# Differential attention in a fused two-block kernel: a head's sum of squares put on all partitions by one product with ones, and a wide root on ScalarE

## The chip, the cores and the metric

The kernel runs on one core of a Trainium2 chip. The metric is the device time of one execution in microseconds (us). Engines are named as in the profile: PE is TensorE (PEld its weight loads), DVE is VectorE, ACT is ScalarE, POOL is GpSimd, SP is SyncE, which issues the weight transfers.

## What is computed

Two blocks of a model on 512 tokens and 1024 channels. The first has a pooling, a gated recurrence and a stick-breaking attention branch and a feed-forward part. The second has two layers; the first of them mixes a state-space branch and a differential attention with 8 heads of width 128. The change is inside this differential attention:

```python
def diff_attention_group(q, k, v, pos, layer, lambdas, subln):
    ...
    def block(start, q1b, q2b):
        mask = chunk_causal_mask(start, s)
        p1 = masked_softmax(jnp.einsum('bqhd,bkhd->bhqk', q1b, k1, ...) * scale, mask)
        p2 = masked_softmax(jnp.einsum('bqhd,bkhd->bhqk', q2b, k2, ...) * scale, mask)
        return jnp.einsum('bhqk,bkhe->bqhe', p1 - lam * p2, vf)

    o = sweep_query_blocks(block, q[:, :, :, 0], q[:, :, :, 1])
    o = rms_norm_2(o, subln) * (1.0 - lam_init)
```

`rms_norm_2` divides each token's 128 values of a head by the root of their mean square. That norm of `o` is what is changed.

## The kernel before

All engines run programs written out by hand; each instruction order is fixed, and engines meet at counted semaphores. Dense products are fp32 work made of three TensorE products of split operands (`L617`, `L618`, `L619`; for value tiles `L638` to `L640`). Every weight panel goes SP transfer, ScalarE cast to `w_hi` (`L1290`, in `hi_to`), GpSimd subtraction to `w_lo` (`L588`, two instructions for a panel of 1024 columns), TensorE.

In the differential attention there are 32 steps c, four query blocks i = 0 to 3 for each of 8 heads. On TensorE (`attend_diff`) a step is: some units of the dense "fill" (the projections of later heads, then the output product `out2a`), the score products of step c + 1 (`L970`, `L973`), more fill, the transposes of step c (`L1015`). Scores of c + 1 wait for ScalarE's exponentials of step c. VectorE takes maxima (`L2304`, `L2305`), ScalarE the exponentials (`L1594`), VectorE normalises and subtracts (`L2338` to `L2341`), then does what the fill has finished (`beside_diff`: rotary products `L2258`, `L2260`, `L2261`, or `L2316`, `L2318` for `out2a`), then the next maxima.

A head's output is made during the steps of the next head, head numbers 0 to 7 here:

- step i = 0: `value_sums` on TensorE (`L984`) writes the head's output, channels on partitions and 512 tokens along the row, into PSUM bank 7. It waits until the head before has left the bank (`s_yb`). ScalarE squares it into `T[:, 0]` (`L1602`) and copies it to `T[:, 1]` (`L1606`).
- step i = 1: `square_sum` (`L992`): for each of four blocks of tokens a product whose held operand is the 128 x 128 block of squares and whose moving operand is one column of ones, so that a sum stands on its token's partition, 128 x 4 in all. ScalarE, in `head_root`, turns them into 1/root by Ln and Exp on 128 x 4 (`L1612`, `L1613`), in `cols`.
- step i = 2: `root_spread` (`L998`): four products of a column of `cols`, repeated, with the identity. They put the 1/root of every token on all partitions, in bank 7.
- step i = 3: `head_out` on VectorE: `L2309` multiplies `T[:, 1]` with a column and with bank 7, and `split` (`L1843`, `L1844`) rounds the result into the two operands of `out2b`.

Head 7 has no next head; after step 31 TensorE does `value_sums(7)`, three units of fill, `square_sum(7)`, three units, `root_spread(7)`, the rest of the fill, and then `out2b`, whose first two tiles wait for banks that VectorE frees at `L2317` after `L2316` and, in their last unit, for head 7's split.

Of the kernel before, what the change touches and what calls it, by code (L numbers as in the profile page):

```python
# [12 lines left out]
ACT = mybir.ActivationFunctionType  # L13
AX = mybir.AxisListType

P = 128
# [3 lines left out]
ST = S // P  # L20
# [211 lines left out]
def run(fill, n):  # L232

    for _ in range(n):
        if next(fill, fill) is fill:
            return
# [19 lines left out]
def build(nc, xt, weights, vectors, late, consts, masks, w_gates, positions, out):  # L256

    ctx = ExitStack()
    with ctx:
# [3 lines left out]
        def sem(name):  # L263
            return ctx.enter_context(nc.semaphore(name))
# [10 lines left out]
        T = sb("T", [P, 4, S])  # L275
# [3 lines left out]
        small = sb("small", [P, 256])  # L279
        cols = sb("cols", [P, 24])  # L280
# [11 lines left out]
        ps = ctx.enter_context(nc.psum_tensor("ps", [P, 8, S], F32))  # L292
# [5 lines left out]
        def con(name, rows=slice(0, P)):  # L298
            at, n = CCOL[name]
            return C_[rows, at:at + n]  # L300
# [151 lines left out]
        def lvec(name, i=0, n=1):  # L452
# [47 lines left out]
        s_ang, s_sin = sem("angles_ready"), sem("sines_ready")  # L500
        s_qc, s_vd, s_rot, s_rotf, s_roped = (sem("qk_copied"), sem("v_copied"), sem("rotated"), sem("rotated_read"),
                                              sem("roped"))
        s_sc, s_mx, s_ex, s_pn, s_tr, s_pt, s_dv, s_osq, s_os, s_or, s_osp, s_og, s_yb = (
            sem("scores_ready"), sem("max_ready"), sem("exp_ready"), sem("probs_ready"), sem("probs_turned"),
            sem("probs_copied"), sem("dv_ready"), sem("o_squares"), sem("o_sum"),
            sem("o_rms"), sem("o_spread"), sem("o_copied"), sem("y_diff_ready"))
        s_s5p, s_s5a, s_s5t, s_s5w, s_bu, s_buf, s_tab, s_tabx, s_ys, s_s5z = (
            sem("s5_params"), sem("s5_params_act"), sem("s5_turned"), sem("s5_in_weights"), sem("bu_ready"),
            sem("bu_read"), sem("table_angles"), sem("tables_ready"), sem("s5_out_ready"),
# [91 lines left out]
        def _(pe):  # L601
            mm_ = nc.tensor.matmul
# [105 lines left out]
            fill = token_units(("v_a", 0), HX)  # L708
# [4 lines left out]
            fill = token_units(("v_a", 1), HX)  # L713
# [228 lines left out]
            fill = chain(fill_dqkv(0), fill_dqkv(1))  # L942
            segments(0)
            for s in range(32):
                pair, i = divmod(s, 4)
# [42 lines left out]
            def square_sum(head):  # L988
                pe.wait_ge(s_osq, head + 1)
                pe.wait_ge(s_og, head + 1)  # L990
                for b in range(ST):
                    mm = mm_(ps[:, 7, b:b + 1], T[:, 0, P * b:P * b + P], con("ones")[:, 0:1], start=True, stop=True)  # L992
                mm.then_inc(s_os, 1)

            def root_spread(head):
                pe.wait_ge(s_or, head + 1)
                for b in range(ST):
                    mm = mm_(ps[:, 7, P * b:P * b + P], cols[:, 12 + b:13 + b].to_broadcast([P, P]), con("ident"),  # L998
                             start=True, stop=True)
                mm.then_inc(s_osp, 1)  # L1000

            def attend_diff(fill):
                scores(0)
                for c in range(32):
                    head, i = c // 4, c % 4
                    n = DIFF_FILL[c % len(DIFF_FILL)]
                    run(fill, n // 2)
                    if c + 1 < 32:
                        scores(c + 1)
                    run(fill, n - n // 2)  # L1010
                    pe.wait_ge(s_pn, c + 1)
                    if c:
                        pe.wait_ge(s_pt, c)
                    for kb in range(i + 1):
                        mm = nc.tensor.transpose(ps[:, 6, P * kb:P * kb + P], EX[:, 2 * (c % 2), P * kb:P * kb + P],  # L1015
                                                 con("ident"))
                    mm.then_inc(s_tr, 1)
                    if i == 0 and head:
                        value_sums(head - 1)
                    if i == 1 and head:  # L1020
                        square_sum(head - 1)
                    if i == 2 and head:
                        root_spread(head - 1)

            def fill_out():
                pe.wait_ge(s_ya, 8)
# [7 lines left out]
            value_sums(7)  # L1034
            run(fill, 3)
            square_sum(7)
            run(fill, 3)
            root_spread(7)
            run(fill, 1000)
            together("out2b", (0, 1), YB, (s_yb, 0))  # L1040
            for t in range(2, 8):
# [198 lines left out]
            fill = fill_mla()  # L1240
# [40 lines left out]
        def _(act):  # L1281
# [316 lines left out]
            def head_squares(head):  # L1598
                act.wait_ge(s_dv, head + 1)
                if head:  # L1600
                    act.wait_ge(s_os, head)
                link(A_(T[:, 0, :], ps[:, 7, :], ACT.Square))  # L1602
                act.sem_inc(s_osq, 1)
                if head:
                    act.wait_ge(s_yb, head)
                link(nc.scalar.copy(T[:, 1, :], ps[:, 7, :]))  # L1606
                act.sem_inc(s_og, 1)

            def head_root(head):

                act.wait_ge(s_os, head + 1)
                link(A_(cols[:, 12:16], ps[:, 7, 0:4], ACT.Ln, bias=con("eps"), scale=1.0 / P))  # L1612
                A_(cols[:, 12:16], cols[:, 12:16], ACT.Exp, scale=-0.5).then_inc(s_or, 1)  # L1613

            exponentials(0)
            for c in range(32):
# [214 lines left out]
        def _(dve):  # L1831
            link = Link(dve, v_own)
            v = nc.vector
# [471 lines left out]
                v.tensor_scalar(small[:, b:b + 2], small[:, b:b + 2], -0.125, None, ALU.mult).then_inc(s_mx, 1)  # L2305

            def head_out(head):
                dve.wait_ge(s_osp, head + 1)
                link(v.scalar_tensor_tensor(T[:, 3, :], T[:, 1, :], small[:, 63:64], ps[:, 7, :],  # L2309
                                            ALU.mult, ALU.mult))  # L2310
                split(YB, head, T[:, 3, :], s_yb)

# [451 lines left out]
```

## Time and profile before

| | us |
|---|---|
| median of 3 runs | 2564.46 (2559.68 to 2565.71) |
| the profiled execution, its own time | 2565.91 |
| its span, first to last instruction | 2564.1 |
| PE busy | 2482.4 (97%) |
| DVE busy | 1310.1 (51%) |
| ACT busy | 868.5 (34%) |
| POOL busy | 1059.6 (41%) |

The differential attention takes from about 1306 us of the span, with the first maximum, to about 1515 us, with the first product of `out2b`. A time such as 1353.15 below is always us from the span's start. In a timeline row the second number is the duration; "x8" on a TensorE fp32 row counts two records for each product in the code.

### The profile page before, as it was taken

What the parts mean: (1) busy time and instruction counts of PE and PEld (TensorE: products, weight loads), DVE (VectorE), ACT (ScalarE), POOL (GpSimd) and SP (SyncE); (2) the same over time, 40 slices, a digit from 0 to 9 for tenths busy, and PEclk for the clock granted to TensorE, in tenths of its full rate; (3) what the DMA queues carried; (4) which work ended last, traced back from release to release, by engine and by line L of the source; (5) the groups of instructions that cost most, each with busy time, mean ns of one, the idle gap of its engine ahead of it and who ended that gap; (6) DMA issues with size and microseconds to landing.
All of it is one profiled execution on the core that took longest, in us unless ns stands there. A gap on an engine that the chain in (4) does not pass through costs nothing.

```text
span 2564.1 us, 30219 instructions
## 1 busy us (share of the span) xinstructions
PE 2482.4 (97%) x11742; PEld 1982.0 (77%) x11742; DVE 1310.1 (51%) x1960; ACT 868.5 (34%) x1360; POOL 1059.6 (41%) x830
## 2 busy tenths in 40 slices
PE   7999999999999999999989999999999889999998
PEld 6887767888888888876667778888888656788886
DVE  6336687543533321584756655596127855533301
ACT  4453345322322222334444433222224443322221
POOL 4322244544544444453222235454454222544442
PEclk9999999999999999999999999999999989999999
DMA  4212122322322233221111123232231012222232
GB/s 147 66 58 72 56 72 89 99 96 93 103 99 95 94 99 98 92 74 58 58 42 50 50 72 106 99 99 94 93 105 54 28 34 63 98 94 95 96 98 78
DMA packets 62574, 209.45 MB, mean 82 GB/s; under 512 B 6880, under 2 KB 9184, under 8 KB 62304
## 3 DMA queue, kind: packets, MB, share of 16 engines
q1 hardware_dynamic: 61424, 204.11, 24.3%
q10 hardware_dynamic: 1008, 3.41, 0.4%
q8 instruction: 94, 1.54, 0.3%
q14 instruction: 48, 0.39, 0.0%
HBM read 205.39 MB, written 2.10 MB: 81 GB/s over the span
## 4 chain that ended last, share of the span: by engine, by line
PE 86%; DVE 10%; ACT 2%; issue 1%; DMA 0%; DVEq 0%; ACTq 0%; SPq 0%
PE ps L617 24%; PE ps L619 24%; PE ps L618 24%; DVE T L2157 1%; PE ps L638 1%; PE ps L639 1%; PE ps L640 1%; PE ps L956 1%; PE ps L733 1%; ACT A L1594 1%; PE ps L725 1%; PE ps L970 1%; PE ps L984 1%; PE ps L754 1%; PE ps L756 1%
## 5 line engine op out<-in xcount | busy, mean ns | idle before, releaser
L588 POOL TENSOR_TENSOR w_lo<-w_raw,w_hi 128x512 fp32r<-128x512 f32 (+4 forms) x822 | 1049.9, 1301 | 1465.8 <-ACT w_hi L1290 1465.8
L617 PE MATMUL ps<-H,w_hi 128*128 128x512 f32 x1880 | 750.6, 399 | 22.6 <-DVEq L1852 12.9
L619 PE MATMUL ps<-H,w_lo 128*128 128x512 f32 x1880 | 736.5, 392 | 0.0
L618 PE MATMUL ps<-H,w_hi 128*128 128x512 f32 x1880 | 736.0, 391 | 0.0
L1290 ACT CAST w_hi<-w_raw 128x1024 fp32r<-128x1024 f32 (+4 forms) x411 | 403.0, 984 | 526.1 <-DMA w_raw<-in_weights_dram 519.7
L617 PEld LDWEIGHTS ps<-H,w_hi 128*128 128x128 f32 x1880 | 355.7, 189 | 110.4 <-issue 21.3
L617 PE MATMUL ps<-split,w_hi 128*128 128x512 f32 x1034 | 410.4, 397 | 6.9 <-issue 3.7
L619 PEld LDWEIGHTS ps<-H,w_lo 128*128 128x128 f32 x1880 | 355.2, 189 | 75.3
L618 PEld LDWEIGHTS ps<-H,w_hi 128*128 128x128 f32 x1880 | 355.9, 189 | 71.2 <-issue 1.7
L619 PE MATMUL ps<-split,w_lo 128*128 128x512 f32 x1034 | 404.2, 391 | 0.0
L618 PE MATMUL ps<-split,w_hi 128*128 128x512 f32 x1034 | 403.7, 390 | 0.0
L1875 DVE TENSOR_TENSOR T<-ps,R 128x512 f32<-128x512 f32 x164 | 113.4, 692 | 405.3 <-PE ps L619 400.9
L617 PEld LDWEIGHTS ps<-split,w_hi 128*128 128x128 f32 x1034 | 194.9, 189 | 49.9 <-issue 7.7
L619 PEld LDWEIGHTS ps<-split,w_lo 128*128 128x128 f32 x1034 | 194.8, 188 | 41.3
L618 PEld LDWEIGHTS ps<-split,w_hi 128*128 128x128 f32 x1034 | 195.0, 189 | 40.0 <-issue 1.4
L1882 DVE TENSOR_TENSOR X<-X,ps 128x512 f32<-128x512 f32 x48 | 33.0, 687 | 331.4 <-PE ps L619 329.8
L1304 ACT ACTIVATE SQ<-X 128x512 f32<-128x512 f32 x49 | 31.0, 632 | 211.7 <-DVEq L1884 198.7
L1477 ACT ACTIVATE T<-T 128x512 f32<-128x512 f32 x66 | 41.7, 632 | 167.7 <-DVEq L2124 167.6
L2127 DVE TENSOR_TENSOR T<-T 128x512 f32<-128x512 f32 x66 | 81.8, 1239 | 9.7
L638 PE MATMUL ps<-w_hi,H 128*128 128x256 f32 x256 | 76.9, 300 | 0.0
L639 PE MATMUL ps<-w_lo,H 128*128 128x256 f32 x256 | 72.7, 284 | 0.0
L640 PE MATMUL ps<-w_hi,H 128*128 128x256 f32 x256 | 72.6, 283 | 0.0
(408 smaller groups left out, 2423.2 us busy)
## 6 DMA issues: line engine op xcount, KB each, us to landing
w_raw<-in_weights_dram SPq DMA_DIRECT2D x323, 512.0 KB, 3.6
w_raw<-in_weights_dram SPq DMA_DIRECT2D x48, 448.0 KB, 3.2
w_raw<-in_weights_dram SPq DMA_DIRECT2D x22, 256.0 KB, 2.6
X<-in_xt_dram SPq DMA_DIRECT2D x4, 512.0 KB, 7.9
out_dram<-A SPq DMA_DIRECT2D x8, 256.0 KB, 2.1
w_raw<-in_weights_dram SPq DMA_DIRECT2D x12, 128.0 KB, 2.0
w_raw<-in_weights_dram SPq DMA_DIRECT2D x6, 192.0 KB, 2.3
A<-in_w_gates_dram ACTq DMA_DIRECT2D x1, 1024.0 KB, 4.8
```

The costliest lines, as they stand in the source:

```text
L588: sub = nc.gpsimd.tensor_tensor(w_lo[:, p % NS, c], w_raw[:, p % NS, c], w_hi[:, p % NS, c].bitcast(F32), ALU.subtract)
L617: mm_(ps[:, bank, :], r(wh), xh, start=(k == 0), stop=False)
L618: mm_(ps[:, bank, :], r(wh), xl, start=False, stop=False)
L619: mm = mm_(ps[:, bank, :], r(wl), xh, start=False, stop=(k == kt - 1))
L638: mm_(o, xh, r(wh), start=(k == 0), stop=False)
L639: mm_(o, xh, r(wl), start=False, stop=False)
L640: mm = mm_(o, xl, r(wh), start=False, stop=(k == kt - 1))
L1290: nc.scalar.copy(w_hi[:, p % NS, 0:PSIZE[p]], w_raw[:, p % NS, 0:PSIZE[p]]).then_inc(w_hi_ready[p % NS], 1)
L1477: A_(T[:, j % 2, :], T[:, j % 2, :], ACT.Silu).then_inc(s_silu, 1)
L1875: link(v.tensor_tensor(dst, ps[:, bank, :], R, ALU.mult))
L1882: link(v.tensor_tensor(X[:, t, :], X[:, t, :], ps[:, bank, :], ALU.add))
L2127: link(v.tensor_tensor(T[:, 2 + q, :], T[:, 2 + q, :], T[:, q, :], ALU.mult))
```

## The change

`square_sum` becomes one product: the held operand is the 128 x 128 block of ones, the moving operand the 512 columns of squares. Every partition then has the sum of every token. ScalarE's Ln and Exp work on 128 x 512, in place in `T[:, 0]`. `root_spread` and its semaphore are gone, and `head_out` reads the root from `T[:, 0]` in SBUF, not from PSUM. Since `T[:, 0]` now lives until `head_out`, `head_squares` waits for `s_yb` before its first instruction; `value_sums`, which it waits for anyway, has already waited for the same count.

```diff
             def square_sum(head):
                 pe.wait_ge(s_osq, head + 1)
                 pe.wait_ge(s_og, head + 1)
-                for b in range(ST):
-                    mm = mm_(ps[:, 7, b:b + 1], T[:, 0, P * b:P * b + P], con("ones")[:, 0:1], start=True, stop=True)
-                mm.then_inc(s_os, 1)
-
-            def root_spread(head):
-                pe.wait_ge(s_or, head + 1)
-                for b in range(ST):
-                    mm = mm_(ps[:, 7, P * b:P * b + P], cols[:, 12 + b:13 + b].to_broadcast([P, P]), con("ident"),
-                             start=True, stop=True)
-                mm.then_inc(s_osp, 1)
+                mm_(ps[:, 7, :], con("ones"), T[:, 0, :], start=True, stop=True).then_inc(s_os, 1)
...
                     if i == 1 and head:
                         square_sum(head - 1)
-                    if i == 2 and head:
-                        root_spread(head - 1)
...
             square_sum(7)
-            run(fill, 3)
-            root_spread(7)
             run(fill, 1000)
...
             def head_squares(head):
                 act.wait_ge(s_dv, head + 1)
                 if head:
-                    act.wait_ge(s_os, head)
+                    act.wait_ge(s_yb, head)
                 link(A_(T[:, 0, :], ps[:, 7, :], ACT.Square))
                 act.sem_inc(s_osq, 1)
-                if head:
-                    act.wait_ge(s_yb, head)
...
                 act.wait_ge(s_os, head + 1)
-                link(A_(cols[:, 12:16], ps[:, 7, 0:4], ACT.Ln, bias=con("eps"), scale=1.0 / P))
-                A_(cols[:, 12:16], cols[:, 12:16], ACT.Exp, scale=-0.5).then_inc(s_or, 1)
+                link(A_(T[:, 0, :], ps[:, 7, :], ACT.Ln, bias=con("eps"), scale=1.0 / P))
+                A_(T[:, 0, :], T[:, 0, :], ACT.Exp, scale=-0.5).then_inc(s_or, 1)
...
             def head_out(head):
-                dve.wait_ge(s_osp, head + 1)
-                link(v.scalar_tensor_tensor(T[:, 3, :], T[:, 1, :], small[:, 63:64], ps[:, 7, :],
+                dve.wait_ge(s_or, head + 1)
+                link(v.scalar_tensor_tensor(T[:, 3, :], T[:, 1, :], small[:, 63:64], T[:, 0, :],
                                             ALU.mult, ALU.mult))
```

TensorE's program at two places of one head in the second half, the sum of squares and, a step later, the place where the root was spread (`C_` holds the constants, the changed kernel's lines are numbered lower):

```order
 L618 MATMUL ps<-H,w_hi 128x512
 L619 MATMUL ps<-H,w_lo 128x512
-L1015 MATMUL ps<-C_,A 128x128 x2
-L992 MATMUL ps<-C_,T 128x1 x4
+L1006 MATMUL ps<-C_,A 128x128 x2
+L991 MATMUL ps<-T,C_ 128x512
...
-L1015 MATMUL ps<-C_,A 128x128 x3
-L998 MATMUL ps<-C_,cols 128x128 x4
+L1006 MATMUL ps<-C_,A 128x128 x3
```

Four products of one column become one of 512 columns, the four of the spread go, and nothing else on TensorE moves.

ScalarE's program before, around head 1's root, with what is queued behind it up to the next exponentials:

```order
576 L1594 ACTIVATE A,small<-ps,small 128x384 x2
577 L1625 COPY A<-ps 128x2x128
578 L1612 ACTIVATE cols<-ps,C_ 128x4
579 L1613 ACTIVATE cols<-cols 128x4
580 L1290 CAST w_hi<-w_raw 128x1024
581 L1354 ACTIVATE A<-ps,cols 128x256 x4
582 L1290 CAST w_hi<-w_raw 128x1024
583 L1594 ACTIVATE A,small<-ps,small 128x512 x2
```

and the same rows of the changed kernel:

```order
576 L1581 ACTIVATE A,small<-ps,small 128x384 x2
577 L1610 COPY A<-ps 128x2x128
578 L1597 ACTIVATE T<-ps,C_ 128x512
579 L1598 ACTIVATE T<-T 128x512
580 L1277 CAST w_hi<-w_raw 128x1024
581 L1341 ACTIVATE A<-ps,cols 128x256 x4
582 L1277 CAST w_hi<-w_raw 128x1024
583 L1581 ACTIVATE A,small<-ps,small 128x512 x2
```

The order is the same; two instructions of 4 columns have 512.

VectorE's program of the changed kernel from head 6's output on, at the end of the attention:

```order
1056 L2303 TENSOR_TENSOR X<-X,A 128x512
1057 L2294 SCALAR_TENSOR_TENSOR T<-T,small 128x512
1058 L1828 CAST split_5253<-T 128x512
1059 L1829 TENSOR_TENSOR split_5235<-T,split_5253 128x512
1060 L2301 TENSOR_TENSOR A<-ps,R 128x512
1061 L2303 TENSOR_TENSOR X<-X,A 128x512
1062 L2294 SCALAR_TENSOR_TENSOR T<-T,small 128x512
1063 L1828 CAST split_5262<-T 128x512
1064 L1829 TENSOR_TENSOR split_5244<-T,split_5262 128x512
1065 L2301 TENSOR_TENSOR A<-ps,R 128x512
```

Only the operands of rows 1057 and 1062 differ from before: there `ps` was read as well, now both tensors are in `T`, in SBUF.

## Rows read from the trace of the kernel before

**Rows 1.** The page, part 4: who holds the chain that ended last

```profile
PE 86%; DVE 10%; ACT 2%; issue 1%; DMA 0%; DVEq 0%; ACTq 0%; SPq 0%
```

**Rows 2.** Timeline of TensorE, heads 0 and 1: start, duration, line, shape

```profile
1345.80 1.02 PE L906 MATMUL ps<-A,C_ 128*128 128x512 f32 x2
1346.65 0.38 PE L1015 MATMUL ps<-C_,A 128*128 128x128 f32 x2
...
1353.15 1.06 PE L998 MATMUL ps<-C_,cols 128*128 128x128 f32 x8
1353.96 0.36 PE L638 MATMUL ps<-w_hi,H 128*128 128x256 f32 x1
```

**Rows 3.** The chain in order of time: head 2's square sum

```profile
1394.20 0.79 PE ps L992 x8
```

**Rows 4.** ScalarE: head 0's root in the timeline

```profile
1348.37 0.27 ACT L1612 ACTIVATE cols<-ps,C_ 128x4 f32<-128x4 f32 x1
1348.67 0.20 ACT L1613 ACTIVATE cols<-cols 128x4 f32<-128x4 f32 x1
```

**Rows 5.** ScalarE lines of width 512: ns min/median/max

```profile
L1309 ACT ACTIVATE R<-ps,C_ x3: 688/688/688, 689.9 to 2202.5; 128x512 f32<-128x512 f32 x3
L1477 ACT ACTIVATE T<-T x66: 631/632/635, 695.0 to 2426.4; 128x512 f32<-128x512 f32 x66
```

**Rows 6.** Timeline, head 0: GpSimd, VectorE, and TensorE's next scores

```profile
1350.66 3.15 POOL L588 TENSOR_TENSOR w_lo<-w_raw,w_hi 128x512 fp32r<-128x512 f32 x2 [8.21 <-ACT w_hi L1290]
1351.01 1.67 DVE L2261 TENSOR_TENSOR A<-A 128x512 f32<-128x512 f32 x1
1356.34 0.49 PE L970 MATMUL ps<-A 64*128 64x128 f32 x4 [0.70 <-ACTq L1596]
```

**Rows 7.** Timeline, head 1: ScalarE's exponentials and TensorE's next scores

```profile
1377.24 0.68 ACT L1594 ACTIVATE A<-ps,small 128x512 f32<-128x512 f32 x1
1378.71 0.19 ACT L1594 ACTIVATION_READ_ACCUMULATOR A<-ps,small 128x1 f32 x1
1379.58 0.49 PE L970 MATMUL ps<-A 64*128 64x128 f32 x4
```

**Rows 8.** Timeline, heads 2, 3 and 4: TensorE's scores after the spread

```profile
1409.22 0.70 PE L970 MATMUL ps<-A 64*128 64x256 f32 x4 [1.67 <-ACTq L1596]
1427.77 0.49 PE L970 MATMUL ps<-A 64*128 64x128 f32 x4
1456.68 0.70 PE L970 MATMUL ps<-A 64*128 64x256 f32 x4 [0.31 <-ACTq L1596]
```

**Rows 9.** Timeline, head 5: GpSimd, VectorE, and TensorE's next scores

```profile
1469.42 2.98 POOL L588 TENSOR_TENSOR w_lo<-w_raw,w_hi 128x512 fp32r<-128x512 f32 x2 [8.03 <-ACT w_hi L1290]
1469.81 1.44 DVE L2318 TENSOR_TENSOR X<-X,A 128x512 f32<-128x512 f32 x1
1474.79 0.49 PE L970 MATMUL ps<-A 64*128 64x128 f32 x4
```

**Rows 10.** Timeline after the attention: L1851 beside GpSimd; the line's ns

```profile
L1851 DVE SCALAR_TENSOR_TENSOR H<-X,V_,H x48: 750/752/1819, 8.2 to 2194.9; 128x512 fp32r<-128x512 f32 x48
1527.16 2.73 POOL L588 TENSOR_TENSOR w_lo<-w_raw,w_hi 128x512 fp32r<-128x512 f32 x2 [14.43 <-ACT w_hi L1290]
1528.77 1.67 DVE L1851 SCALAR_TENSOR_TENSOR H<-X,V_,H 128x512 fp32r<-128x512 f32 x1
```

**Rows 11.** Timeline, head 6's output and the value sums that wait for it

```profile
1498.54 2.98 POOL L588 TENSOR_TENSOR w_lo<-w_raw,w_hi 128x512 fp32r<-128x512 f32 x2 [8.43 <-ACT w_hi L1290]
1500.42 0.75 DVE L2309 SCALAR_TENSOR_TENSOR T<-T,small,ps 128x512 f32<-128x512 f32 x1
1502.73 2.39 PE L984 MATMUL ps<-A 128*128 128x512 f32 x8 [1.82 <-DVEq L1845]
```

**Rows 12.** Timeline, head 7 up to the first product of out2b

```profile
1507.69 5.03 POOL L588 TENSOR_TENSOR w_lo<-w_raw,w_hi 128x512 fp32r<-128x512 f32 x4 [6.18 <-ACT w_hi L1290]
1508.47 0.26 ACT L1612 ACTIVATE cols<-ps,C_ 128x4 f32<-128x4 f32 x1
1511.21 0.75 DVE L2309 SCALAR_TENSOR_TENSOR T<-T,small,ps 128x512 f32<-128x512 f32 x1 [7.01 <-PE ps L998]
1514.68 0.50 PE L617 MATMUL ps<-split,w_hi 128*128 128x512 f32 x1 [1.53 <-DVEq L2317]
```

More of the change, by code:

```diff
@@ L502, in build @@
                                               sem("roped"))
-        s_sc, s_mx, s_ex, s_pn, s_tr, s_pt, s_dv, s_osq, s_os, s_or, s_osp, s_og, s_yb = (
+        s_sc, s_mx, s_ex, s_pn, s_tr, s_pt, s_dv, s_osq, s_os, s_or, s_og, s_yb = (
             sem("scores_ready"), sem("max_ready"), sem("exp_ready"), sem("probs_ready"), sem("probs_turned"),
             sem("probs_copied"), sem("dv_ready"), sem("o_squares"), sem("o_sum"),
-            sem("o_rms"), sem("o_spread"), sem("o_copied"), sem("y_diff_ready"))
+            sem("o_rms"), sem("o_copied"), sem("y_diff_ready"))
         s_s5p, s_s5a, s_s5t, s_s5w, s_bu, s_buf, s_tab, s_tabx, s_ys, s_s5z = (
```

## The prediction, made before the changed kernel ran

> **What bounds the kernel now.** I read the page first: TensorE holds 86% of the chain that ended last, VectorE 10% [rows 1]. The question for each head is therefore whether TensorE or the loop from scores over VectorE's maxima and ScalarE's exponentials back to the next scores ends last at the place where an instruction is taken away. The timeline of TensorE shows this at the scores L970: where the row names a wait for ScalarE's queue, the loop is late and TensorE is early; where it names none, TensorE itself is the bound. I went through the eight heads this way, and looked in the timelines of ScalarE, VectorE and GpSimd at what the longer root delays.
>
> **TensorE, the two prices.** The spread of a head starts at 1353.15 and the next product at 1353.96: 0.81 us are removed [rows 2]. The square sum takes 0.79 now [rows 3]. Its successor is one fp32 product with 512 moving columns and a held 128 x 128 operand of constants; the nearest row is the rotation L906, of the same form, which starts at 1345.80 and lets the next start at 1346.65, so 0.85 [rows 2]. That adds 0.06. Where TensorE is the bound a head gains 0.81 - 0.06 = 0.75.
>
> **ScalarE.** Ln and Exp of 128 x 4 take 0.27 and 0.20 [rows 4]. For the wide ones the rows of the same width and operands are the root L1309 out of PSUM with a bias, 0.69, and L1477 in SBUF, 0.63 [rows 5]. So 0.42 and 0.43 more, 0.85 a head, for all that is queued behind. No table of functions changes, since the exponentials around use the same Ln and Exp set.
>
> **VectorE.** L2309 reads one tensor in SBUF and one in PSUM now, and takes 0.75 even while GpSimd works [rows 11]. Afterwards both are in SBUF. The row of that form is L1851: 0.75 as a rule, and 1.67 when it starts inside one of GpSimd's subtractions, because it waits for the end of the one that is running [rows 10]. So the price is 0 where GpSimd is idle and up to 0.92 where it is not. In this trace L2309 starts well inside GpSimd's work for two heads, 6 and 7, the two where VectorE's output is on the path [rows 11, 12].
>
> The Trainium skill, page "SBUF — State Buffer", section "SBUF: two separate sides", states this as a rule: a VectorE instruction with two SBUF inputs and a GpSimd instruction that reads SBUF exclude each other for the whole instruction. The trace agrees, with 1.67 against 0.75 [rows 10]. Without the rule the sum below would be 2563.8 less the stalls of heads 6 and 7, the third rival below.
>
> **Head by head.** Head 0: TensorE waits 0.70 before its next scores already, so the removal alone would only lengthen that wait. But behind ScalarE's root stand a copy and the weight cast that releases GpSimd at 1350.66, and VectorE's L2261, issued at 1351.01, waits for GpSimd: 1.67 instead of about 0.7 [rows 6]. With the cast 0.85 later GpSimd starts at 1351.51, after L2261 has begun. The loop is then 1.0 shorter, and TensorE, 0.75 earlier by itself with 0.70 of wait in hand, can follow. I take -1.0; the bounds are 0, if GpSimd still comes first, and -1.4.
>
> Head 1: ScalarE goes without a pause from the root over a cast, four row copies and another cast into the exponentials at 1377.24, which end at 1378.90; the scores follow at 1379.58 with no wait [rows 7]. With 0.85 the exponentials end at 1379.75, and with the 0.1 that a release takes, the scores start at 1379.85. TensorE would have been ready at 1378.8. So +0.3 in place of -0.75.
>
> Head 2: TensorE waits 1.67 at 1409.22, for a loop that began with scores before the spread [rows 8]; the gain goes into the wait, and the 0.06 of the longer sum remains: +0.1. Head 3: no wait at 1427.77 [rows 8], ScalarE and VectorE idle before it: -0.75. Head 4: the scores at 1456.68 wait 0.31 for a loop that began earlier [rows 8]; 0. Head 5: L2318 is 1.44 because GpSimd, released by the cast behind the root, started at 1469.42, 0.39 before it [rows 9]. The later cast turns the order round as in head 0 and frees 0.75 in the loop; TensorE's scores at 1474.79, without a wait but just behind the exponentials, come 0.75 earlier by both counts. I take -0.75, with bounds 0 and -0.8.
>
> Head 6: after the removed spread TensorE waits 1.82 for VectorE's output of head 6 before value_sums(7) [rows 11]. The removal adds to that wait. The scalar product at 1500.42 lies inside GpSimd's second subtraction, which ends at 1501.52 [rows 11]. It will wait for that end: 1.0, less 0.15 that the rounding behind it spends in the same stall now. +0.9 with the longer sum.
>
> Head 7: ScalarE's two casts end as before, so the root starts at 1508.47 as it does now [rows 12], and ends, 0.69 + 0.03 + 0.63 later, at 1509.8. VectorE can start 1.4 earlier than 1511.21. But GpSimd has four subtractions of 1.26 from 1507.69 to 1512.72 [rows 12], and scalar product, rounding and subtraction of the split all can stall behind one each: the first starts at 1510.2 and ends at 1510.9, the second starts at 1512.1, the third at 1513.7 and ends at 1514.4; L2316 follows and frees the bank at 1515.2, against TensorE's first product at 1514.68 [rows 12]. +0.6. If the three run through together once the first has the port, it is -1.5 instead.
>
> **The sum.** -1.0 + 0.3 + 0.1 - 0.75 + 0 - 0.75 + 0.9 + 0.6 = -0.6 us on the span of 2564.1. Behind the attention nothing is touched; TensorE is without a wait there. The profiled execution took 2565.91, 1.45 above the median of 2564.46; on the median I forecast 2563.8.
>
> **The rivals.** First, TensorE alone decides: each of seven heads gives 0.75, and the end gives 1.4 plus nothing for stalls: -6.7, 2557.8. For it speaks the 86%; against it the waits of 0.70, 1.67, 0.31 and 1.82 at heads 0, 2, 4 and 6 [rows 6, 8, 11]. Even this stays within 0.3% of the time, which is 7.7 us.
>
> Second, the other side: the new scalar product, now a reader of two SBUF tensors, meets GpSimd at every head and is on the path at every head, 8 x 0.92 = 7.4, while the wide root costs head 1 0.3 and swallows the rest of the gains: +7.7, about 2572. It decides from the point where GpSimd's subtractions cover L2309 in most heads and VectorE has no pause behind it. Against it: in six of eight heads L2309 does not start inside one, and the next maxima stand ahead of it in VectorE's program, so its delay reaches only the step after.
>
> Third, the scalar product does not stall at heads 6 and 7: the 0.85 of head 6 goes, head 7 gives -1.4 in place of +0.6: -3.4, 2561.0. L2309 itself, unstalled at 0.75 inside GpSimd's work, speaks for it, L1851 against it [rows 10, 11].
>
> Fourth, the turned order of GpSimd and VectorE at heads 0 and 5 does not come about, since a tenth of a microsecond moves such meetings, and TensorE's wait swallows the removal: head 0 gives 0 and head 5 0: +1.1, 2565.6.
>
> **Chances and range.** The likeliest sum 0.55, the third 0.13, the fourth 0.2, the first 0.08, the second 0.04. A measurement of this kernel tells apart about 0.3%, 7.7 us, and the three runs of before lie 6 us apart, more than all likely sums. The range reaches from the first rival to somewhat above the fourth with half of that scatter: 2558 to 2568. Faster by over 0.3%: 0.03, from the first rival together with a low run. Slower: 0.03, the second. Within 0.3%: 0.94.
>
> **What the profile of after would show.** The square sum with 0.85 from its start to the next; Ln 0.69 and Exp 0.63; the scores after head 1's root behind a wait for ScalarE; L2261 of head 0 and L2318 of head 5 at 0.7; the scalar products of heads 6 and 7 at 1.1 to 1.9 and those of heads 0 to 5 at 0.75; a wait of about 3.5 in place of 1.82 before value_sums(7), and a wait of 2 to 3 before the first product of out2b. Wrong would make it a wide root much slower than 1.35 in all, or a shift of GpSimd that puts new stalls on VectorE's loop in several heads at once.

## The result, and the profile after

The changed kernel takes 2570.07 us, median of 14 runs (2564.88 to 2572.43), against 2564.18 for 14 runs of the kernel before (2559.68 to 2565.91). The ratio is 1.0022, 95% interval 1.0015 to 1.003: 5.9 us slower, where 2563.8 was forecast, 0.4 below this median, and outside the range of 2558 to 2568. (A ratio on record compares all runs of both kernels and need not equal the ratio of the two medians.) A second series of 11 runs of the changed kernel gave 2566.78, against 2564.21 for the kernel before on that chip, ratio 1.0016 (1.0008 to 1.0025). Its profiled execution has a span of 2569.2 us and a mean granted TensorE clock of 0.983; before it was 2564.1 and 0.986.

The page, part 4, of the changed kernel, which answers to [rows 1]: nothing in the shares hints at a cause.

```profile
PE 86%; DVE 10%; ACT 2%; issue 2%; DMA 0%; DVEq 0%; ACTq 0%; SPq 0%
```

ScalarE's wide root, as groups of the attention by form (sum, mean ns); this answers to [rows 5]. The prices are as forecast.

```profile
L1597 ACT ACTIVATE T<-ps,C_ 128x512 f32<-128x512 f32 x8 | 5.5, 693 | 0.2 <-PE ps L991 0.2
L1598 ACT ACTIVATE T<-T 128x512 f32<-128x512 f32 x8 | 5.1, 632 | 0.3
```

Head 1's next scores in TensorE's timeline, which wait 1.14 here, as forecast:

```profile
1377.84 0.49 PE L970 MATMUL ps<-A 64*128 64x128 f32 x4 [1.14 <-ACTq L1583]
```

Head 0 and head 5 in the timelines of VectorE and GpSimd, answering to [rows 6, 9]:

```profile
1349.30 0.69 DVE L2246 TENSOR_TENSOR A<-A 128x512 f32<-128x512 f32 x1
1349.81 2.58 POOL L588 TENSOR_TENSOR w_lo<-w_raw,w_hi 128x512 fp32r<-128x512 f32 x2 [9.08 <-ACT w_hi L1277]
1351.59 0.82 DVE L2290 TENSOR_SCALAR small<-small 128x2 f32<-128x2 f32 x1
...
1470.08 0.69 DVE L2303 TENSOR_TENSOR X<-X,A 128x512 f32<-128x512 f32 x1
1470.54 2.63 POOL L588 TENSOR_TENSOR w_lo<-w_raw,w_hi 128x512 fp32r<-128x512 f32 x2 [8.89 <-ACT w_hi L1277]
1472.26 0.94 DVE L2290 TENSOR_SCALAR small<-small 128x2 f32<-128x2 f32 x1
```

GpSimd now comes after the large instruction, which takes 0.69 and not 1.67 or 1.44. But then it holds up the next one that is open to it, the scaling of two columns, L2290, which takes 0.17 when nothing stands in its way. So the stall has moved, and only a part of the gain, or none, is left.

The end of the attention, answering to [rows 11, 12], and head 2's scores:

```profile
1407.45 1.23 PE L970 MATMUL ps<-A 64*128 64x256 f32 x4 [2.57 <-ACTq L1583]
1500.62 1.63 DVE L2294 SCALAR_TENSOR_TENSOR T<-T,small 128x512 f32<-128x512 f32 x1
1503.65 4.60 PE L984 MATMUL ps<-A 128*128 128x512 f32 x8 [3.43 <-DVEq L1830]
1513.36 1.79 DVE L2294 SCALAR_TENSOR_TENSOR T<-T,small 128x512 f32<-128x512 f32 x1 [8.23 <-ACT T L1598]
1518.25 0.50 PE L617 MATMUL ps<-split,w_hi 128*128 128x512 f32 x1 [2.29 <-DVEq L2302]
```

Here is what the forecast did not have. The waits are as forecast, 3.43 before value_sums(7) (about 3.5) and 2.29 before out2b (2 to 3), but the products behind them are slow. The first scores after the wait of 2.57 take 1.23, not 0.70; the eight records of the value sums take 4.60, not 2.39. The windows of the changed kernel (length, then busy time of PE, PEld, DVE, ACT, POOL, then TensorE's granted clock, the share of the DMA engines and GB/s) show what is slow:

```profile
1407.00:1414.00 7.00, 6.55 (x19) 4.57 (x20) 5.03 (x15) 2.15 (x8) 0.00 (x0) 0.51 0.27 77
1503.00:1510.00 7.00, 6.35 (x14) 4.17 (x15) 1.83 (x3) 1.49 (x3) 0.00 (x0) 0.54 0.00 0
1519.00:1524.00 5.00, 5.00 (x16) 3.95 (x15) 0.00 (x0) 0.00 (x0) 0.00 (x0) 0.66 0.00 0
```

And in the kernel before, in the two corresponding stretches, with waits of 1.67 and 1.82 ahead of them:

```profile
1408.00:1415.00 7.00, 5.78 (x29) 4.04 (x30) 5.15 (x16) 2.97 (x11) 0.00 (x0) 1.00 0.25 75
1502.00:1509.00 7.00, 6.27 (x30) 4.94 (x31) 1.91 (x3) 3.54 (x6) 1.31 (x2) 1.00 0.17 61
```

A value of 1.00 is 2.4 GHz, and 0.51 is 1.2 GHz nearly throughout. From the scores at 1409.22 to the next the kernel before takes 7.02 us, the changed one 10.02; from value_sums(7) to the square sum 4.31 and 7.16; behind the first product of out2b 1.58 more are lost. These three come to 7.4 us, and the attention is 6.8 longer from its first scores to the stretch after it. The spans of the two profiles differ by 5.1 only, because 1.7 us were won before the attention, where the profile of before has 3.4 us more at 1.2 GHz, at 95 us.

The kernel before has the same pattern once in its own attention, at its longest wait there, before the second scores:

```profile
1308.23 0.70 PE L970 MATMUL ps<-A 64*128 64x256 f32 x4 [2.91 <-ACTq L1596]
```

```profile
1305.00:1313.00 8.00, 5.09 (x23) 4.00 (x22) 4.70 (x16) 2.05 (x8) 0.00 (x0) 0.80 0.06 11
```

### The profile page after: what moved, and what is told of

Read it like the earlier page. It is cut to its first block, busy times and chain, and to the rows that moved or that the text cites. A ratio compares the mean times of both kernels' runs of the same rounds, so it can differ in the third digit from the quotient of the medians.

```text
span 2569.2 us, 29995 instructions
## 1 busy us (share of the span) xinstructions
PE 2481.7 (97%) x11630; PEld 1974.7 (77%) x11630; DVE 1305.5 (51%) x1960; ACT 875.6 (34%) x1360; POOL 1058.7 (41%) x830
## 4 chain that ended last, share of the span: by engine, by line
PE 86%; DVE 10%; ACT 2%; issue 2%; DMA 0%; DVEq 0%; ACTq 0%; SPq 0%
PE ps L617 24%; PE ps L619 24%; PE ps L618 23%; DVE T L2142 1%; PE ps L638 1%; PE ps L639 1%; PE ps L640 1%; ACT A L1581 1%; PE ps L956 1%; PE ps L733 1%; PE ps L984 1%; DVE small L2289 1%; PE ps L725 1%; PE ps L754 1%; PE ps L970 1%
```

## The experiments

All were compared with the kernel before on the same chip. Beside the time I read two things: the mean clock of every run, and the median of time times clock, about what a run would take at 2.4 GHz throughout. The clock is on record to 0.001, which is 2.6 us of that product for one run, so differences of 1 or 2 us in it are weak.

A profile is one execution, and its later stages vary too. So here is, for the profiles on which the argument rests, what lies in the attention and what does not: the starts of four VectorE instructions, the same ones in every kernel (`L2274`, `L1856`, `L2572` and `L1875` of the kernel before), and the two lengths between them that differ.

| profile | attention's start | behind it | later | later still | attention | 2110 to 2300 |
|---|---|---|---|---|---|---|
| before | 1300.31 | 1560.24 | 2110.74 | 2300.43 | 259.93 | 189.69 |
| changed | 1298.66 | 1565.39 | 2115.93 | 2305.51 | 266.73 | 189.58 |
| changed, again (9) | 1300.37 | 1562.45 | 2112.30 | 2297.82 | 262.08 | 185.52 |
| same TensorE work (2) | 1300.34 | 1562.12 | 2111.88 | 2297.41 | 261.78 | 185.53 |
| three groups (14) | 1298.03 | 1557.65 | 2108.24 | 2297.93 | 259.62 | 189.69 |

The last column has two levels, some 4.2 us apart. At the lower one (the short form below) the profiles have 3.4 and 3.4 us at 1.2 GHz there, at the higher one 10.2 and 6.8. No edit touches that stage.

**1. The spread alone taken away.** Narrow square sum and narrow root stay; the output lacks the heads' norm.

```diff
-            def root_spread(head): ...
...
-                    if i == 2 and head:
-                        root_spread(head - 1)
...
-            run(fill, 3)
-            root_spread(7)
...
             def head_out(head):
-                dve.wait_ge(s_osp, head + 1)
+                dve.wait_ge(s_or, head + 1)
```

> The kernel before without the four spread products of each head, all else kept: narrow square sum, narrow root, VectorE multiplies with bank 7 in PSUM, where nothing puts the root (so the heads' norm is left out of the output). Clock theory: the slowdown comes from TensorE's longer waits, after which its granted clock falls to 1.2 GHz. The wait before the scores of step 12 grows from 1.67 to about 2.5 and the one before value_sums(7) from 1.82 to about 2.6; at least one of them is followed by 6.8 us at 1.2 GHz that the kernel before has not, some 3 us each. Time against before -3 to +3, and not the saving of 5 to 6. Rival theory, the stalls of VectorE and the longer root on ScalarE make the slowdown: this kernel has neither, so it is faster than before by 2 to 6 us, with no new stretch at 1.2 GHz.

Measured: 2558.47 against 2563.75, ratio 0.9978 (0.997 to 0.9987), clock 0.988. The waits grew as said, 2.56 and 2.71, but in the profiled run neither was followed by the low clock. TensorE's timeline at head 2's scores, and the windows there:

```profile
1409.69 0.49 PE L970 MATMUL ps<-A 64*128 64x256 f32 x2 [2.56 <-ACTq L1585]
```

```profile
1407.00:1414.00 7.00, 4.44 (x22) 2.89 (x22) 5.04 (x15) 2.63 (x9) 0.01 (x1) 1.00 0.21 67
```

So a wait of 2.6 can be followed by the low clock and need not be. But head 0's wait, 0.70 before, had grown to 1.60 at 1355.83, and behind it this profile has 3.4 us at 1.2 GHz that the kernel before has not (clock 0.57 from 1357 to 1361). Removing TensorE work alone can thus bring the low clock; it did not make this kernel slower.

**2. The changed kernel with TensorE's old amount of work.**

```diff
+            def idle_products(head):
+                pe.wait_ge(s_or, head + 1)
+                for b in range(ST):
+                    mm_(ps[:, 7, P * b:P * b + P], con("ones"), con("ident"), start=True, stop=True)
...
+                    if i == 2 and head:
+                        idle_products(head - 1)
```

> The changed kernel with four products of constants of the old spread's size put into bank 7 at the old spread's place in every head, results unused. Wide root and the product of two SBUF tensors stay. Clock theory: head 2's wait goes back to about 1.7 and is not followed by the low clock, which takes 3 us away, but each head where TensorE is the bound costs 0.8 again. The wait before value_sums(7) stays at 2.6, because the stalled product makes it, and may still be followed by the low clock. In all 1 to 4 us faster than the changed kernel, +2 to +5 against before. Rival theory, stalls and longer root: nothing of theirs is undone and work is added, so 0 to 5 us slower than the changed kernel, +6 to +11 against before.

Measured: 2563.09 against 2563.75, ratio 0.9995 (0.9986 to 1.0003), clock 0.988, so 7 us below the changed kernel with more work in it, and below the +2 to +5 against before that was expected. In the profiles, which are 7.7 apart, 4.95 lie in the attention, 261.78 against 266.73, and 4.05 in the stage from 2110 to 2300, where this execution had the short form; 1.7 go the other way, ahead of the attention. The 4.95 speak against stalls and longer root as the cause: both are in here in full. They don't show that the whole loss is gone, since the attention is still 1.85 longer than before. Head 2's wait was 1.67 and the clock behind it 1.00; the wait before value_sums(7) was 2.54 with 1.2 GHz behind it in part. The windows of this kernel:

```profile
1407.00:1414.00 7.00, 5.33 (x25) 3.22 (x25) 4.97 (x16) 2.90 (x10) 0.00 (x0) 1.00 0.23 77
1503.00:1509.00 6.00, 5.76 (x17) 4.06 (x18) 1.42 (x3) 1.97 (x3) 0.00 (x0) 0.72 0.01 4
```

**3. The operand in SBUF alone.** The norm is left out of the output.

```diff
-                    act.wait_ge(s_os, head)
+                    act.wait_ge(s_yb, head)
                 link(A_(T[:, 0, :], ps[:, 7, :], ACT.Square))
                 act.sem_inc(s_osq, 1)
-                if head:
-                    act.wait_ge(s_yb, head)
...
-                link(v.scalar_tensor_tensor(T[:, 3, :], T[:, 1, :], small[:, 63:64], ps[:, 7, :],
+                link(v.scalar_tensor_tensor(T[:, 3, :], T[:, 1, :], small[:, 63:64], T[:, 0, :],
```

> The kernel before, in which only the operand of the last product of a head is changed: T[:, 0] in SBUF (the squares, so the norm is left out of the output) and not bank 7. Both theories see the product at head 6 take 1.6 and not 0.75. Clock theory: the wait before value_sums(7) becomes 1.82 + 0.85 = 2.7; if a wait of that length is enough, 1.2 GHz follows and the time is +4 against before, if not +1 to +2. Rival theory, stalls alone: +1 to +2.5 with head 7's stalls.

Measured: 2569.11, ratio 1.0019 (1.0007 to 1.003). The twelve runs fall into six of 2559.9 to 2566.7 and six of 2571.5 to 2574.5. The profiled one belongs to the second kind. It has the wait of 2.55 before value_sums(7) with the low clock behind it, a wait of 2.04 before out2b with 3.4 us of it, and besides 20 us at 1.2 GHz from 1943 us on, in a later stage, which neither the profile of before nor the two of the changed kernel have. Its windows:

```profile
1502.00:1508.00 6.00, 5.11 (x14) 3.45 (x15) 2.07 (x3) 1.13 (x2) 0.00 (x0) 0.72 0.07 26
1943.00:1964.00 21.00, 21.00 (x83) 19.03 (x82) 6.96 (x12) 7.71 (x15) 5.03 (x4) 0.52 0.07 26
```

**4. The longer root alone.**

```diff
                 A_(cols[:, 12:16], cols[:, 12:16], ACT.Exp, scale=-0.5).then_inc(s_or, 1)
+                nc.scalar.copy(T[:, 2, 0:S], T[:, 1, 0:S])
+                nc.scalar.copy(cols[:, 20:24], T[:, 1, 0:4])
```

> The kernel before with one copy of 512 and one of 4 columns behind each head's narrow root on ScalarE, results unused, about as long as the wide root is longer (0.8 us). TensorE's work and VectorE's operand are as before. Clock theory: no new wait above 2, no new stretch at 1.2 GHz, time within 1.5 us of before. Rival theory, the longer root delays exponentials: +0.3 to +1 at head 1 and more if other heads follow, +1 to +6.

Measured: 2564.35, ratio 1.0004 (0.9995 to 1.0013), no new low clock in its profile. The longer root alone costs nothing that these runs can tell.

**5. The root in PSUM.** The changed kernel without its SBUF operand.

```diff
-                A_(T[:, 0, :], T[:, 0, :], ACT.Exp, scale=-0.5).then_inc(s_or, 1)
+                A_(ps[:, 7, :], T[:, 0, :], ACT.Exp, scale=-0.5).then_inc(s_or, 1)
...
-                link(v.scalar_tensor_tensor(T[:, 3, :], T[:, 1, :], small[:, 63:64], T[:, 0, :],
+                link(v.scalar_tensor_tensor(T[:, 3, :], T[:, 1, :], small[:, 63:64], ps[:, 7, :],
```

> The changed kernel with one part undone: the wide Exp writes into bank 7, and VectorE's last product of a head reads PSUM again. Theory now: what turned a neutral change into a slower one is that this product reads two SBUF tensors, stalls behind GpSimd for heads 6 and 7, lengthens TensorE's wait before value_sums(7) to 3.4, and 1.2 GHz follows there. Then the product takes 0.75 in all heads, the wait before value_sums(7) is 2.5 to 2.7, the mean granted clock of a run is 0.986 to 0.989 and not 0.983, and the time is 4 to 9 us below the changed kernel, -3 to +2 against before. Rival: removed TensorE work alone lets the clock fall, by the wait of 2.5 at head 2, whatever VectorE reads; then the clock stays at 0.983 to 0.985 and the time within 2 us of the changed kernel, +4 to +6 against before.

Measured: 2573.41 in 5 runs, ratio 1.0035 (1.0023 to 1.0047), clock 0.982. My theory that the operand is what counts fell. The product took 0.75 and the wait before value_sums(7) was 2.70, and the low clock came behind both waits all the same (and behind one of 2.19 before out2b), and for 24 us from 1942 on as in the third. Behind a wait of 2.93 before the second scores it did not come.

```profile
1406.31 1.23 PE L970 MATMUL ps<-A 64*128 64x256 f32 x4 [2.57 <-ACTq L1583]
1501.86 4.02 PE L984 MATMUL ps<-A 128*128 128x512 f32 x8 [2.70 <-DVEq L1830]
```

Time times clock is 2526.6, the lowest of all, so the loss is in the clock, and more of it in the stretch from 1942 on than in the attention.

**6 to 8. Products of constants in the waits, badly placed.** `keep_busy(n, copied)` before scores or value sums issues n products of ones with the identity into bank 6. It waits first until the bank is read, and as written it did so ahead of every step's scores, n = 0 included. The sixth is the changed kernel with three such groups, the first of them at c = 11, which is not the step whose scores wait 2.57; the seventh the kernel before with one, `{0: 12}`; the eighth the fifth with four, `{0: 12, 11: 11}` and the two at the end.

```diff
+            def keep_busy(n, copied):
+                if copied:
+                    pe.wait_ge(s_pt, copied)
+                for b in range(n):
+                    mm_(ps[:, 6, P * (b % 4):P * (b % 4) + P], con("ones"), con("ident"), start=True, stop=True)
...
+                    keep_busy({11: 11}.get(c, 0), c)
                     if c + 1 < 32:
                         scores(c + 1)
...
+            keep_busy(14, 32)
             value_sums(7)
...
+            keep_busy(12, 32)
             together("out2b", (0, 1), YB, (s_yb, 0))
```

> The changed kernel, nothing undone, with products of constants whose results are unused where TensorE waits anyway: 11 before the scores that wait 2.57, 14 before value_sums(7) that waits 3.43, 12 before the first product of out2b that waits 2.29 (0.2 us each). Theory: the granted clock falls because TensorE stands still. Then no stretch at 1.2 GHz follows these three places, mean clock 0.986 to 0.989, time 4 to 9 us below the changed kernel although work is added. Rival: the low clock is a matter of the run and not of the waits, and the stalls alone cost the time; then nothing is gained, or 1 us lost, against the changed kernel.

> The kernel before with 12 products of constants at the one place of the attention where its clock falls too: before the second scores, which wait 2.9 for ScalarE. Theory: the 6.8 us at 1.2 GHz behind it go, 2 to 4 us faster than before. Rival: the clock falls there all the same, or is made up elsewhere: within 1 us of before.

> The changed kernel with the root in PSUM (as e5) and products of constants in all four long waits (as e6 and e7 together). Theory: no stretch at 1.2 GHz in the attention at all, mean clock 0.988 to 0.991, 8 to 13 us below the changed kernel, -3 to -8 against before, the fastest so far. Rival, that the waits do not set the clock: no better than e5.

Measured: 2574.81 (ratio 1.0048, 1.0032 to 1.0064), 2562.80 (1.0007, 0.9995 to 1.0019) and 2576.35 (1.004, 1.0027 to 1.0052). Time times clock rose to 2536.7, 2533.5 and 2535.6, since the added wait held up scores that had waited for nothing: in the sixth's profile those at 1460.00 wait 1.00 for a copy. All three expectations of the time failed. In the seventh eight runs lie at 2560.6 to 2563.0 and four at 2570.6 to 2573.3, and all three profiles have 20 to 24 us at 1.2 GHz from 1942 to 1947 on. In the attention no low clock stands where a group filled the wait (before value_sums(7) and out2b in the sixth and eighth, before the second scores in the seventh and eighth), but it came behind waits of 1.76, 2.29, 3.21 and 3.22 elsewhere. The times don't tell the theories apart, and the runs were made again.

**9. The changed kernel again**, with no edit.

> The changed kernel itself once more, for a second profile and more times. What stands after eight runs: time multiplied by the mean granted clock, that is about the time at full clock, is 2 us lower than before (2527.4 against 2529.6), and TensorE is at 1.2 GHz for 82 us of a run and not for 67 to 72. If the low clock belongs to the changed kernel's waits, the second profile has it again behind the waits before the scores at 1407 and before value_sums(7), the median is again 5 to 7 above before, and the mean clock 0.984. If it is chance between executions, the profile has it elsewhere and the median moves by several us.

Measured: 2566.78, as above, 2.6 over before; clock 0.985; the median moved by 3 us between the series. The expectation, if the loss belongs to the kernel, was 5 to 7 over before, so the size of the loss was not repeated. The profiled run is the fastest of the eleven, 2563.66, and has the short form of the stage from 2110 to 2300. It has the low clock at the same two places, by its windows, but none behind its wait of 2.86 before the second scores and none behind that of 2.26 before out2b, and its attention is 2.15 longer than before, not 6.8:

```profile
1404.00:1413.00 9.00, 7.03 (x20) 4.73 (x21) 6.90 (x20) 2.89 (x10) 0.00 (x0) 0.62 0.19 60
1500.00:1508.00 8.00, 5.73 (x12) 3.65 (x13) 3.38 (x5) 0.98 (x2) 0.33 (x1) 0.59 0.13 51
```

**10. No spread and a longer root**, the edits of 1 and 4 together; the heads' norm is left out.

```diff
...
-                    if i == 2 and head:
-                        root_spread(head - 1)
...
+                nc.scalar.copy(T[:, 2, 0:S], T[:, 1, 0:S])
+                nc.scalar.copy(cols[:, 20:24], T[:, 1, 0:4])
```

> The first experiment's kernel (no spread products, narrow sum and root, the norm left out of the output) with a copy of 512 and one of 4 columns behind each root on ScalarE, so two of the three parts of the change together. The part alone without the spread was -5.3, the longer root alone +0.6. If the low clock comes of two parts together, as the root in PSUM with +9 lets one think, the time is +4 to +10 against before with a mean clock of 0.982 to 0.985. If the parts only add, -5 to -3 with a clock of 0.988.

Measured: 2560.59, ratio 0.9984 (0.9975 to 0.9993), clock 0.988: the parts about add. So these two parts together, longer waits included, do not make a kernel slower either. Its waits of 2.56 and 2.70 had the low clock behind them, which those of the first experiment had not.

**11 and 12. Products in the waits, without the fault.**

```diff
+            def keep_busy(n, root):
+                if root:
+                    pe.wait_ge(s_or, root)
+                for b in range(n):
+                    mm_(ps[:, 7, P * (b % 4):P * (b % 4) + P], con("ones"), con("ident"), start=True, stop=True)
...
+                    if c == 0:
+                        keep_busy(12, 0)
+                    if c == 11:
+                        keep_busy(11, 2)
                     if c + 1 < 32:
                         scores(c + 1)
...
+            keep_busy(15, 7)
             value_sums(7)
...
+            keep_busy(10, 8)
             together("out2b", (0, 1), YB, (s_yb, 0))
```

> The sixth experiment again without its fault, a semaphore wait that it added before every step's scores. The changed kernel with products of constants into bank 7 in the four long waits of TensorE in the attention: 12 before the second scores, 11 before the scores of step 12, 15 before value_sums(7), 10 before out2b. If standing still lets the clock fall there, the profile has no 1.2 GHz between 1300 and 1525 and that part is 5 to 10 us shorter than the changed kernel's; the total is 5 to 10 lower too unless a later part loses it again. If not, the low clock is still there.

> The seventh experiment again without the added wait: the kernel before with 12 products of constants in the 2.9 us wait before the second scores. In the attention the 6.8 us of 1.2 GHz behind that wait go and 3 us with them. In the time, 3 us less in the runs that have no long stretch of low clock near 1942 us, 8 more in those that have; the seventh experiment had 8 runs of the first kind and 4 of the second.

Measured: the changed kernel 2559.13, ratio 0.9986 (0.9978 to 0.9995); the kernel before, with only the group at c = 0, 2559.60, ratio 0.9981 (0.9972 to 0.999). Both beat both originals. With 12 products in the 2.91 us wait of the kernel before, the wait left is 0.16 and the clock 1.00; its attention is 3.3 shorter in the profile. The twelfth's timeline of TensorE there, L1006 being the 12 products (two records each), and its windows:

```profile
1303.66 2.84 PE L1006 MATMUL ps<-C_ 128*128 128x128 f32 x24
1306.66 0.70 PE L970 MATMUL ps<-A 64*128 64x256 f32 x4 [0.16 <-ACTq L1604]
```

```profile
1300.00:1313.00 13.00, 12.84 (x75) 10.80 (x74) 7.28 (x17) 2.85 (x11) 2.73 (x2) 1.00 0.15 52
```

In the eleventh one group stood at the wrong step, before scores that wait 1.1, and the low clock at 1406 remained for 3.4 us.

**13 and 14. The group set right**, with the one at c = 0 and, in the fourteenth, without it.

```diff
-                    if c == 11:
-                        keep_busy(11, 2)
+                    if c == 16:
+                        keep_busy(11, 3)
```

> The eleventh experiment with the second group of products where it was meant to be. It stood before the scores of step 12, which wait 1.1, and not before those of step 17, which wait 2.57 at 1409; there 3.4 us of low clock had remained at 1406. Now four groups: before the second scores, before those of step 17, before value_sums(7) and before out2b. Standing still as the cause: no 1.2 GHz at all between 1300 and 1525, and the attention another 2 to 3 us shorter than in the eleventh, time 2555 to 2559. Rival, that the low clock at 1406 has another cause: it stays, and the time is that of the eleventh or above.

> As the thirteenth, without the group before the second scores, where the kernel before has its low clock as well: the changed kernel with products of constants only in the three waits that are longer, or new, through the change. Standing still as the cause of the slowdown: the time is that of the kernel before less the forecast saving, 2561 to 2565, with a mean clock of 0.986 to 0.988, against 2570 and 2567 for the changed kernel. Rival: 2566 to 2571.

Measured: with four groups 2561.28, ratio 0.9988 (0.998 to 0.9997), above the 2555 to 2559 expected; one run, the profiled one, at 2555.1. With the three groups in the waits that the change made longer, 2563.48 against 2563.38, ratio 0.9996 (0.9987 to 1.0005), mean clock 0.986 in both. Its windows at the places where the changed kernel had 0.51 and 0.54:

```profile
1404.00:1413.00 9.00, 8.88 (x56) 6.91 (x55) 6.88 (x19) 3.38 (x11) 0.14 (x1) 1.00 0.20 60
1500.00:1508.00 8.00, 7.99 (x32) 5.83 (x33) 2.10 (x3) 4.40 (x6) 3.03 (x3) 1.00 0.01 2
```

The slowdown is gone while every part of the change is still there. This is the cleanest comparison of two profiles: the fourteenth and the changed kernel have the same length from 2110 to 2300, 189.69 and 189.58, and the attention is 259.62 against 266.73, 7.1 shorter, with products added. Four groups make no low clock in the attention at all, but the median is 2 above the eleventh's; a few us are won or lost in the later stages.

## Why the prediction was wrong

**The prices** were right: Ln 0.69, Exp 0.63, the scalar product 0.75 for heads 0 to 5 and 1.63 and 1.79 for heads 6 and 7. The wide square sum cost nothing measurable: the scores behind head 0's sum start 1.74 earlier than before, as those of the step ahead did within 0.04.

**The sum of work and waits** was right, by partly wrong terms. Against the kernel before, and without the stretches at 1.2 GHz, the changed kernel's profile gives -0.3 at head 0 (forecast -1.0), +0.3 at head 1 (+0.3), -0.9 at head 3 (-0.75), 0 at heads 2 and 4, -0.05 at head 5 (-0.75), +0.7 at head 6 (+0.9) and -0.2 at the end (+0.6). The sum is -0.5, against -0.6. That the two sums agree so well is luck: heads 0 and 5 give 1.4 less than forecast, and the end 0.8 more. Time times clock is lower in both series, 2527.4 in the first, where no clocks of the kernel before are on record (it has 2529.1 to 2529.8 in the later series), and 2528.4 against 2529.1 in the second.

Head 0 and head 5 failed in one step: "with the cast 0.85 later GpSimd starts at 1351.51, after L2261 has begun" came true, but not that the loop is then 1.0 shorter. The small L2290 was caught in place of the large instruction. I asked which instruction the shifted one would no longer meet, and not which it would meet next. The end was +0.6 in the forecast because three stalls follow one another; two did, the product with 1.79 and the rounding with 1.39, while the subtraction took its plain 0.69. But the clock moved GpSimd and root apart, so that this term can't be checked on its own. In the fourteenth experiment, at full clock, heads 6 and 7 together cost 0.8, its added products included, against a forecast of 1.5.

**The step that failed** is the treatment of a wait as a place that costs nothing: "TensorE waits 1.67 ...; the gain goes into the wait", "the removal adds to that wait". That is right as long as the clock stays. The waits grew from 1.67 to 2.57 and from 1.82 to 3.43, as computed, and TensorE came out of them at 1.2 GHz. The sentence that begins "Wrong would make it" did not name it either, although the trace of before shows the pattern at its own longest wait of the attention, the 2.91 before the second scores. I had read the clock only as a mean.

The Trainium skill, page "TensorE: Matmul & The Clock Gate", section "HAM oscillation — how this bites in real kernels", describes this pattern: TensorE waits for an operand, and the next products run at half clock. The trace agrees in the pattern, with clocks of 0.51 and 0.54 behind the waits of 2.57 and 3.43. The page's case has a wait in every round of a loop; here single waits do it.

What shows the cause is the fourteenth experiment: it fills only the lengthened waits, and its median is 0.1 us over that of the kernel before beside it, where the two series of the changed kernel were 5.9 and 2.6 over theirs; in its profile the loss is gone from the attention. The second experiment restores TensorE's work and supports this, with a median 0.7 under the kernel before, but part of that lies in the short form of a later stage.

**What stays open.** Length alone does not decide. In the sixteen profiles the attention has 26 waits of 2.5 us or more, and the clock falls within 1.7 us of the end of 21 of them; it does at four of five between 2.0 and 2.3, and at three of 34 between 1.5 and 1.82 (1.60 in the first experiment, 1.76 in the sixth and eighth). The same wait of 2.56 was followed by it in the tenth's profile and not in the first's. The 20 to 24 us at 1.2 GHz from about 1942 in the profiles of the third and of the fifth to eighth, worth some 10 us, lie in a stage that no edit touches; why some kernels have them, by their times, in most or all runs and others in none wasn't settled. The 4.2 us between the two forms of the stage from 2110 to 2300 are open in the same way. So the size of a kernel's median, within some 5 us, depends on something beyond the attention, and that the changed kernel lost 5.9 in one series and 2.6 in the other fits this, and was not taken apart further.

## What to carry to other kernels

Where TensorE waits already, work taken from it is not free: it lengthens the wait, and at 21 of the 26 waits of 2.5 us or more the next products ran at half clock, up to 3 us lost each time. When an edit puts its saving into a wait, read the granted clock behind the waits of that length that the trace has, and cost the lengthened one by them; a dozen products of constants in the longest wait of the kernel before gave 4.6 us, of which the profile shows 3.3 in the attention. When a shift frees an instruction from a stall, look for the next one that will meet the same neighbour.

## What was not expected of the hardware

- The clock after waits of TensorE in the attention: 1.67 and 1.82, 1.00 in the profile of before; 2.54 and 2.55, 0.72 over 6 us; 2.57 and 3.43, 0.51 and 0.54 over 7 us; but 2.56, 1.00 in one profile, and 1.60, 0.57 over 4 us in the same one.
- A VectorE scaling of 128 x 2, 0.17 by itself, takes 0.82 and 0.94 when it starts inside a GpSimd subtraction. It ends 0.02 to 0.03 after the subtraction does, so even so small an instruction waits for the end of a large one.
- Executions of one kernel differ by up to 14.6 us while the work is the same, from 2559.9 at 0.990 to 2574.5 at 0.982 in the third experiment; time times clock is 2534 and 2528.
